# One inference step of a two-layer trunk: the flag's branch one expert turn earlier, and the last unit of both output projections taken accumulator by accumulator

## The reference

```python
h = rms_norm(x, norm_mix[layer])
x = x + mixer(h)                    # layer 0: forgetting attention and gated DeltaNet, then w_out_even
                                    # layer 1: gated MLP over positions, then w_out_odd
h = rms_norm(x, norm_ffn[layer])
x = x + hier_moe(h)                 # 32 experts of width 256, two per token, of one group of 8

def hier_moe(h, ...):
    g_sel = argmax(h @ w_rg)                      # one of 4 groups
    top_v, top_i = top_k((h @ w_re)[g_sel], 2)    # two of its 8 experts
    gates = softmax(group)[g_sel] * softmax(top_v)
    return sum over the two experts: gate * (silu(h @ w_gate) * (h @ w_up)) @ w_down
```

## Time and profile before

| | us |
|---|---|
| three runs: median, lowest, highest | 1193.15, 1190.41, 1194.59 |
| the profiled execution | 1194.03 |
| its span in the trace | 1192.4 |
| PE busy | 1064.2 (89%) |
| DVE busy | 428.3 (36%) |
| ACT busy | 233.9 (20%) |
| output projection of layer 0 ends, first router product | 436.61, 442.74 |
| turns of layer 0, first gate_up to end of the last additions | 465 to 706 |
| output projection of layer 1 ends, first router product | 922.42, 926.16 |
| turns of layer 1 | 949 to 1185 |
| bytes read | 292.46 MB |

### The profile page before, as it was taken

The page is one execution under the profiler, slowest core; times in us unless marked ns, Lnnn a source line. Parts: engine busy times, 40 slices in busy tenths (PEclk is TensorE's granted clock), DMA queues, the critical chain, the costliest instruction groups (busy, mean ns, idle before and its releaser), DMA issues.

```text
span 1192.4 us, 17155 instructions
## 1 busy us (share of the span) xinstructions
PE 1064.2 (89%) x6728; PEld 619.7 (52%) x6728; DVE 428.3 (36%) x1092; ACT 233.9 (20%) x495; POOL 88.8 (7%) x199
## 2 busy tenths in 40 slices
PE   8999997776698999899897799999999998978786
PEld 7777676464598446444343334444444654434332
DVE  2723354242575434433252320034001434334334
ACT  2321133333400113111000022131100411100002
POOL 6334040040000000000000000000000000000000
PEclk9899999898799999999899899999999999999898
DMA  9760284783800158999999875335323979999992
GB/s 295 190 180 4 68 254 125 201 283 143 320 33 1 52 169 353 383 421 421 421 420 421 370 231 184 124 115 212 119 101 110 384 288 422 420 421 422 421 419 102
DMA packets 87718, 298.83 MB, mean 251 GB/s; under 512 B 16067, under 2 KB 52475, under 8 KB 57902
## 3 DMA queue, kind: packets, MB, share of 16 engines
q1 hardware_dynamic: 73172, 273.92, 60.0%
q0 software_dynamic: 5152, 17.05, 4.7%
q10 hardware_dynamic: 9306, 6.67, 1.8%
HBM read 292.46 MB, written 5.16 MB: 250 GB/s over the span
## 4 chain that ended last, share of the span: by engine, by line
PE 69%; DMA 15%; DVE 8%; issue 3%; ACT 2%; SPq 2%; ACTq 0%; DVEq 0%
DMA arena<-in_moe_w_up 14%; PE ps L1334 9%; PE ps L761 9%; PE ps L1153 9%; PE ps L1139 6%; PE ps L1424 5%; PE ps L721 2%; PE ps L1186 2%; PE ps L1203 2%; PE ps L712 2%; PE ps L926 1%; PE ps L1327 1%; PE ps L992 1%; PE ps L983 1%; PE ps L990 1%
## 5 line engine op out<-in xcount | busy, mean ns | idle before, releaser
L1139 PE MATMUL ps<-lvl,htok 128*128 128x128 f32 (+3 forms) x768 | 139.3, 310 | 7.5 <-DVE x L2220 7.5
L1153 PE MATMUL ps<-arena,hT 128*32 128x512 f32 x1024 | 123.5, 630 | 25.1 <-DMA arena<-in_moe_w_up 25.1
L1139 PEld LDWEIGHTS ps<-lvl,htok 128*128 128x128 f32 (+1 forms) x768 | 105.3, 188 | 49.5 <-issue 16.5
L761 PE MATMUL ps<-hT,arena 128*128 128x288 f32 x448 | 114.5, 418 | 0.0
L1334 PE MATMUL ps<-arena,hT 128*128 128x512 f32 x256 | 111.0, 593 | 0.0
L761 PEld LDWEIGHTS ps<-hT,arena 128*128 128x128 f32 x448 | 86.8, 195 | 26.9 <-issue 1.7
L1153 PEld LDWEIGHTS ps<-arena,hT 128*32 128x32 f32 x1024 | 34.2, 115 | 100.7 <-issue 99.1
L1203 PE MATMUL ps<-arena 128*128 128x512 f32 x128 | 71.7, 689 | 15.4 <-DVE x L2214 15.4
L1334 PEld LDWEIGHTS ps<-arena,hT 128*128 128x128 f32 x256 | 48.3, 190 | 59.7 <-issue 59.7
L2206 DVE TENSOR_SCALAR hT<-ps,nw 128x128 f32<-128x128 f32 (+1 forms) x64 | 22.7, 355 | 111.0 <-PE ps L1139 110.8
L1186 PE MATMUL ps<-arena 128*32 128x512 f32 x512 | 58.2, 595 | 1.3 <-ACT arena L1676 1.3
(11 more groups left out here) (437 smaller groups left out, 1277.7 us busy)
## 6 DMA issues: line engine op xcount, KB each, us to landing
arena<-in_moe_w_gate SPq DMA_DIRECT2D x66, 1024.0 KB, 19.0
arena<-in_moe_w_up SPq DMA_DIRECT2D x66, 1024.0 KB, 20.9
arena<-in_moe_w_down SPq DMA_DIRECT2D x66, 1024.0 KB, 23.0
arena<-in_cache_k SPq DMA_DIRECT2D x64, 256.0 KB, 3.4
arena<-in_cache_v POOLq DMA_DIRECT2D x64, 256.0 KB, 3.6
arena<-in_w_in_odd SPq DMA_DIRECT2D x16, 1024.0 KB, 11.1
arena<-in_w_in_even SPq DMA_DIRECT2D x14, 1024.0 KB, 8.5
arena<-in_w_out_odd SPq DMA_DIRECT2D x8, 1024.0 KB, 7.8
```

What stands on the lines that cost most here:

```text
L761: last = mm(ps[:, c % 4, 0:T], w[:, k, P * (c % 2):P * (c % 2 + 1)], hT[:, k, :], start=k == 0, stop=k == KD - 1)
L1139: last = mm(ps[:, row_bank(k), 0:w], htok[0:m, i, P * k:P * (k + 1)], pl[0:m, i, 0:w], start=i == 0, stop=i == 2)
L1153: last = mm(ps[EC * j:EC * (j + 1), q % 2, :], xgT[q % 2][:, k, EC * j:EC * (j + 1)], ring[:, sl:sl + 2, DE * k:DE * (k + 1)], start=k == ...
```

## The change

**The branch.** `FLAG_TURN` goes, and `SPLIT = NQ - 2` = 6 comes. PE, ACT and DVE run turns 0 to 5 ahead of the branch instead of 0 to 6, read the flag behind turn 4, and both arms hold turns 6 and 7. The turns themselves stay as they are.

**The last unit of the output projections.** In layer 0 the state products 4 to 7 all come behind `out_proj(2, 1)`, and the fourth unit is done by a new function `out_last`: first the samples' accumulator with both inner blocks, then each prompt bank with both, and a count on `gm_o_ps` after each of the five. Layer 1's last unit is done by the same function. DVE's `add_out` follows the accumulators in this order for both layers, so the tiles of `x` are complete in the order samples, rows 0, rows 1 (`ROWS_FIRST`).

**Into the experts.** The first `spin` goes. PE transposes samples and rows 0 of blocks 0 to 2 (`EARLY`) when two tiles are complete, and rows 1 behind it when the third is. The transposes use banks 5, 6, 7 and 0 (`x_bank`), since banks 0 to 3 still hold sums. ACT squares in the new order and copies block 3 ahead of the last tile's square. SP's waits for the slots of the last units follow the new counts.

```diff
-        FLAG_TURN = NQ - 3
+        SPLIT = NQ - 2
...
+        EARLY = 3
+
+        def x_bank(k):
+
+            return (5, 6, 7, 0)[k % 4]
...
                 if u < 14:
                     sp.wait_ge(s.proj_ps, 2 * (u + 1))
+                elif u < 17:
+                    sp.wait_ge(s.w_used, u - 13)
                 else:
-                    sp.wait_ge(s.w_used, u - 13)
+                    sp.wait_ge(s.gm_o_ps, 5)
...
-            def transpose_k(n, k):
+            def transpose_k(n, k, tiles=ROWS_FIRST):
                 if k >= 4:
                     hT_copied(n, k - 4)
-                for i, (r0, m) in enumerate(TOK):
-                    last = tr(ps[:, k % 4, r0:r0 + m], x[0:m, i, k::KD], ident[0:m, 0:m])
-                last.then_inc(s.hT_ps, 1)
+                for i in tiles:
+                    r0, m = TOK[i]
+                    last = tr(ps[:, x_bank(k), r0:r0 + m], x[0:m, i, k::KD], ident[0:m, 0:m])
+                if 1 in tiles:
+                    last.then_inc(s.hT_ps, 1)
...
+            def out_last(lhs, w, c0, stop_sem):
+
+                for e in range(2):
+                    for qr in range(4):
+                        last = mm(ps[TS * qr:TS * (qr + 1), 4, 0:QC], lhs[:, c0 + e, TP:T],
+                                  w[:, e, QC * qr:QC * (qr + 1)], start=False, stop=e == 1)
+                last.then_inc(stop_sem, 1)
+                for b in range(4):
+                    for e in range(2):
+                        last = mm(ps[:, b, :], lhs[:, c0 + e, P * (b // 2):P * (b // 2 + 1)],
+                                  w[:, e, 512 * (b % 2):512 * (b % 2 + 1)], start=False, stop=e == 1)
+                    last.then_inc(stop_sem, 1)
...
-            for n in range(4):
-                out_proj(2 + n // 2, n % 2)
-                if n < 3:
-                    state_change(2 * n + 2)
-                    state_change(2 * n + 3)
+            out_proj(2, 0)
+            state_change(2)
+            state_change(3)
+            out_proj(2, 1)
+            for j in range(4, 8):
+                state_change(j)
+            wait_even(pe, 17)
+            out_last(mixT, cview(17), 6, s.gm_o_ps)
...
-                spin(5, 8 if layer == 0 else 4)
+                pe.wait_ge(s.x_new, 3 * n - 1)
+                for k in range(EARLY):
+                    transpose_k(n, k, ROWS_FIRST[0:2])
                 pe.wait_ge(s.x_new, 3 * n)
...
-                        transpose_k(n, k)
+                        transpose_k(n, k, ROWS_FIRST[2:] if k < EARLY else ROWS_FIRST)
...
-                        for q in range(NQ - 1):
+                        for q in range(SPLIT):
                             turn(q)
-                            if ask and q == FLAG_TURN:
+                            if ask and q == SPLIT - 2:
                                 ask()
                     else:
-                        turn(NQ - 1)
+                        for q in range(SPLIT, NQ):
+                            turn(q)
                         out_rows(NQ - 1)
...
-            out_rows(HC - 1)
+            wait_odd(pe, 23)
+            pe.wait_ge(s.gm_t, NU)
+            out_last(uT, oview(23), NU - 2, s.gm_o_ps)
             moe(1, 3)
...
             def norm_stats(n_):
-                for i in range(3):
-                    act.wait_ge(s.x_new, 3 * (n_ - 1) + i + 1)
-                    if i:
-                        hT_odd(n_, 2 * i - 1)
+                for j, i in enumerate(ROWS_FIRST):
+                    act.wait_ge(s.x_new, 3 * (n_ - 1) + j + 1)
+                    if j == 2:
+                        hT_odd(n_, 1)
+                        hT_odd(n_, 3)
                     square(n_, i)
...
-            act.wait_ge(s.gm_o_ps, 5)
+            act.wait_ge(s.gm_o_ps, 10)
             moe(1, 3)
...
-            def add_out(used):
-                dve.wait_ge(s.w_used, used)
-                for i in range(2):
-                    for hf in range(2):
-                        last = V.tensor_tensor(x[:, i, 512 * hf:512 * (hf + 1)], x[:, i, 512 * hf:512 * (hf + 1)],
-                                               ps[:, 2 * i + hf, :], ALU.add)
-                    last.then_inc(s.x_new, 1)
+            def add_out(n):
+                dve.wait_ge(s.gm_o_ps, 5 * n + 1)
                 for qr in range(4):
                     xs = x[0:TS, 2, QC * qr:QC * (qr + 1)]
                     last = V.tensor_tensor(xs, xs, ps[TS * qr:TS * (qr + 1), 4, 0:QC], ALU.add)
                 last.then_inc(s.x_new, 1)
+                for b in range(4):
+                    dve.wait_ge(s.gm_o_ps, 5 * n + b + 2)
+                    xs = x[:, b // 2, 512 * (b % 2):512 * (b % 2 + 1)]
+                    last = V.tensor_tensor(xs, xs, ps[:, b, :], ALU.add)
+                    if b % 2:
+                        last.then_inc(s.x_new, 1)
```

49 lines of the change are left out of this document (18 added, 31 removed).

## The result

The changed kernel took 1182.7 us (median) against 1194.6 us for the kernel before on the same chip: a ratio of 0.989, 95% interval 0.986 to 0.992 (time after over time before; the forecast's 1.018 is the other way round, and 1.011 was measured in its terms). Two later sessions gave 0.991 (0.988 to 0.994) and 0.989 (0.985 to 0.992). The profiled execution took 1180.45 us with a span of 1178.5 us; that of before had 1192.4. One of the five executions took 1271.0 us at a granted clock of 0.82 instead of 0.95 and is left out of the ratio. The granted clock is the profile's column for TensorE's clock, as a share of its full speed.

What follows compares the result with a forecast made beforehand. Memory rate (420 to 422 GB/s) and TensorE could both be the limit, with local waits deciding. Gains of 3.2 + 9.8 + 1.7 + 6.3 = 21.0 us from 1193.15 gave 1172.2 us, range 1166 to 1181.

Steps and rivals of the forecast that it cites:

- Branch, the wait it moves under: Before turn 6, both layers: TensorE's 3.5 us stop and DVE's 4.84 and 3.45 us hide in existing waits.
- "Cost nothing" for the branch in turn 6: Before gate_up(6): TensorE's stop ends at 642.5, weights come at 644.25, leaving 1.7 us of cover in each layer.
- rival (a): Turn 6 or 7: the branch's stop is not hidden, 3.5 us a stop, 1176 to 1180 us in all; chance 0.19.
- D: Stretch from gate_up(0) of layer 1 to its down(7), forecast at 220.6 us.
- Turn 7: gate_up(7) 5.9 us after down(6); down(7) earlier by 9.8 us in layer 0, 6.3 us in layer 1.
- B: Stretch from gate_up(0) of layer 0 to its down(7), forecast at 221.5 us.
- Output projection, layer 0: Reordered last unit: 0.9 us lost at the second state pair, first router product at 439.55 instead of 442.74, gain 3.2 us.
- (c): Router and gate_up(0): the clock falls where idle products were removed, making the kernel slower than before; chance 0.03.
- Output projection, layer 1: Last unit with samples first: first router product 2.05 us after the projection's end instead of 3.8, gain 1.7 us.
- C: Stretch from down(7) of layer 0 to gate_up(0) of layer 1, holding layer 1's projection, where 1.7 us were forecast.
- rival (b): Turn 7's weights: the stream is a harder bound, units landing 3 us later, 1177 to 1180 us in all; chance 0.10.

Runs made afterwards that it cites:

- after_third: The changed kernel run a third time, unaltered: 1182.0 us, ratio 0.989 to the kernel before.
- swap_pe1: The changed kernel with the arms of TensorE's branch in layer 1 exchanged, traced only: 179.00 us from gate_up(0) to gate_up(6) of layer 1.
- pad128: The changed kernel with 128 never-executed instructions ahead of TensorE's branch target: layer 1 took 180.00 us from gate_up(0) to gate_up(6), 32.51 on to gate_up(7).
- pad64: The changed kernel with 64 never-executed instructions ahead of TensorE's branch target: layer 1 took 180.13 us from gate_up(0) to gate_up(6), 32.59 on to gate_up(7).
- proj_only: The changed kernel with the branch back ahead of turn 7: 1190.9 us, ratio 0.997 to the kernel before.
- no_branch: The changed kernel without the further-rounds arm, so without the branch on TensorE, ACT and DVE: 1176.9 us, ratio 0.985 to the kernel before.
- after_again: The changed kernel run once more, unaltered: 1183.6 us, ratio 0.991 to the kernel before.
- reorder: The changed kernel with layer 0's second state pair moved behind the last unit's samples' products: 1178.5 us, ratio 0.985 to the kernel before.
- swap_timed: The changed kernel with TensorE's arms in layer 1 exchanged, now timed: 1181.2 us, ratio 0.989 to the kernel before.
- swap_all1: The changed kernel with the arms exchanged on TensorE, DVE and ACT in layer 1: 178.81 us from gate_up(0) to gate_up(6) there.
- fill_wait: The changed kernel with two idle products between the first and second state pair of layer 0: 1182.6 us, ratio 0.989 to the kernel before.
- keep_clock: The changed kernel with exchanged arms, plus idle products in turn 6's weight wait and the spatial stage's two gaps: 1180.9 us, ratio 0.989 to the kernel before.
- split4: The changed kernel with the branch before turn 4: 1180.9 us, ratio 0.989 to the kernel before.

## Why the prediction was wrong, step by step

**Branch, the wait it moves under: right in kind.** TensorE's and DVE's first stops, DVE's second, the flag read a turn earlier: all hidden in the changed kernel's first trace, as said. TensorE's first stop was bare by 0.6 us in after_third, where down(5) ended late.

**"Cost nothing" for the branch in turn 6: the step that failed first.** It counted stops against idle time, and the idle time was there. It did not count that with TensorE's jump there the load that ends this idle time comes later: 5.26 us of it became 6.30, with gate_up(6) 1.0 to 1.2 us later (swap_pe1 against pad128 in layer 1: 179.00 and 180.00). And it put TensorE's second stop aside as rival (a), because TensorE had none in the trace of before. That is a property of the old layout. In the new one it came in layer 1 in each of its three traces and stretched gate_up(6) to 11.4, 12.7 and 15.2 us. Both together took 3.2 to 4.5 us from the 6.3 us of layer 1 (D 223.76 and 225.09, forecast 220.6). In this layout TensorE's two stops of layer 1 end 8.9 to 9.4 us after down(5), where the prediction had 5.3 us of idle time to put one of 3.5 under. The stop went when the target was moved by 64 or 128 instructions (pad64, pad128), so it goes with the place of the target; why this place has it, no run shows. The prediction gave rival (a) a chance of 0.19.

**Turn 7: right.** 5.9 us from down(6)'s end to gate_up(7) was forecast; with down(6)'s 3.64 us that is 9.5 from start to start, and it is 9.33 in every trace with the early turn 7. down(7) of layer 0 waited for the last w_down, as said. B was 221.4 to 222.1 against 221.5 forecast: the 9.8 us came as 9.2 to 10.0.

**Output projection, layer 0: right where the clock stays at 1.00, and wrong about the clock; the second step that failed.** For the second state pair 0.9 us were taken as lost, though the prediction's own 429.4 against 428.1 makes 1.3; the wait was 0.78 us, and the projection ended 1.1 us later after the first pair's start (11.68 us against 10.59). The first router product came 2.32 us after its end, not 2.05, and in all 2.7 us were gained and not 3.2. The first refill of layer 0 was issued at 475.70, 2.4 us earlier and not 3.2. But in 8 of 13 traces the clock fell in that very wait, and the gain was -0.6 us (16.72 to 17.28). In the prediction's chances (c), at 0.03, is the case that the kernel gets slower than before because the clock falls in the router and gate_up(0), where the idle products had been taken away. No run shows its cost. What the changed kernel's trace shows there is a granted clock of 1.00 (442 to 450 us); the danger was in a wait that the same sum had priced at its own length and no more.

**Output projection, layer 1: right.** 1.7 us forecast, 1.98 measured in C of proj_only.

**Not in the sum: the spatial stage.** The prediction put it at nothing without a word; it lost 1.4 to 3.1 us at the lower clock, in a stage that the change doesn't touch. Why is open, as said above.

**The weights as a harder bound, rival (b):** not in itself. Without a branch there (no_branch) the weights of turn 6 came when forecast (178.95 and 179.09 us), and the floor of 219.9 us in D is 0.7 us below what was forecast.

In sum, for a typical trace of the changed kernel with the fall in the projection (after_again): 21.0 forecast, less 3.8 in the projection of layer 0 (3.2 to -0.6), 0.6 in B, 1.4 in C and 4.5 in D: 10.7 us. The medians of the three sessions have 9.8 to 12.9.

## What to carry to other kernels

A jump that is put under a wait for a load must be counted twice: its stop against the idle time (3.5 to 3.8 us here), and the lateness of the load that ends it (1.0 to 1.3 us); and a second stop behind the target (it took gate_up(6) to 11.4 us and more) has to be expected until a trace of the new layout shows none. Where one arm of a condition is the usual one, let it be the arm that follows without a jump, and let the jump fall where the engine has nothing more to do (here D fell from 223.8 or more to 219.9 us, and 0.4 to 1.1 us were paid at the end). A wait of under a microsecond in front of long products isn't priced by its length alone (0.77 us here, and 3.3 us more in 8 of 13 traces): look at the granted clock right behind it in several traces, and fill it with useful work, as reorder did, rather than with idle products that outlast it.

## What the runs showed of the hardware

- The granted clock fell from 1.00 to its lower level, 0.50, after a wait of 0.77 us in 8 traces of 13 (3.3 us lost each time), and after two waits of 0.97 us beside short transposes in 12 of the 13 with an early turn 7 and in none of the 3 with the late one (1.4 to 3.1 us lost). Whether it fell went with the clock of an earlier stretch both times: all 8 of the falls, and none of the 5 others, had 0.50 in the 20.4 us that end 82 us before the first state product. Once down, it stayed down for 27 us of nearly unbroken products in three traces (0.50 in 980 to 1000 us of after_third, with PE busy for 19.55 of the 20), and the weights of turn 6 came 6.5 to 7 us later.
- A taken jump stopped TensorE for 3.5 to 3.6 us in the kernel before (from the end of down(6) to the next pass, 670.2 to 673.70 and 1154.2 to 1157.80) and for 3.84 us in layer 1 of after_third, where the wait for the weights didn't cover it. With the target where the changed kernel has it, or eight instructions further on, it was stopped a second time, and the two stops ended 8.9 to 9.4 us after its last pass before the jump in all five traces of this kind, however much of that a wait for weights covered; with the target 64 or 128 instructions further on there was no second stop.
- With TensorE's jump ahead of turn 6 the last weights of that turn landed about 1 us later in layer 1 (179.5 to 179.8 us after gate_up(0), against 178.4 to 178.7), though only two instruction packets of 16 KB went over q8 in 1112 to 1121 us of the changed kernel (one in swap_pe1); the jumps of DVE and ACT made no such difference (179.00 and 178.81 us in swap_pe1 and swap_timed, 178.81 in swap_all1).
- The same code up to layer 0's first state product took 411.6 to 422.0 us in 18 traces, nearly as much as the whole effect of the change. From gate_up(0) to gate_up(6) of layer 1 the traces without TensorE's jump there have 178.78 to 179.00 us and those with it 179.88 to 180.13, the two with a low clock in turn 1 (after_third, fill_wait), keep_clock and split4 left aside. That made 1 us readable from single traces.
